# The opening of a two-block transformer kernel: modulation weights into fifteen buffers of their own, bias table first, X scaled for all tiles ahead of the shift

## The reference, cut to what matters

```python
def ada_modulation(c, w, b):                       # w: 1024 x 3072
    mod = jax.nn.silu(c) @ w + b
    shift, scale, gate = jnp.split(mod, 3, axis=-1)
    return shift[:, None], scale[:, None], gate[:, None]

shift, scale, gate = ada_modulation(c, ada_w[layer, 0], ada_b[layer, 0])
h = rms_norm(x, norm_w[layer, 0]) * (1.0 + scale) + shift
y = hybrid_attention_mixer(h, attn_w_in[i], ...)   # h @ w_in, then attention with a bias
x = x + (gate * y)                                 # by distance, taken from rel_bias (32 x 8)
```

## Time and profile before

| | |
|---|---|
| median of 3 runs | 956.2 us (955.88 to 959.43) |
| the profiled execution | 958.09 us, of which its span 956.4 us |
| PE busy | 888.4 us (93%) |
| DVE busy | 692.1 us (72%) |
| ACT busy | 456.8 us (48%) |
| DMA engines | mean 206 GB/s |

### The profile page before, as it was taken

How to read it: one execution, slowest core, us unless ns; L and a number is a source line. 1 busy time by engine, 2 the same in 40 slices (tenths; PEclk the granted TensorE clock), 3 DMA queues, 4 the chain that set the end, 5 groups by cost and what they waited for, 6 DMA issues and landing times.

```text
span 956.4 us, 17671 instructions
## 1 busy us (share of the span) xinstructions
PE 888.4 (93%) x7028; PEld 852.6 (89%) x7028; DVE 692.1 (72%) x877; ACT 456.8 (48%) x573; POOL 58.0 (6%) x104
## 2 busy tenths in 40 slices
PE   2599999899999996799999999999999999999996
PEld 1388879799999996699999999988989999999996
DVE  4889878788878888766666556855487877776665
ACT  2347464566643333456663433444465444444445
POOL 2110110211111110000000000000000000000000
PEclk9789999999999996799999999999999999999998
DMA  9895755499989994057765555653435555654531
GB/s 336 300 339 193 244 200 177 130 319 322 317 306 330 330 316 134 23 184 234 239 199 176 175 183 168 197 166 130 157 90 177 177 179 187 218 173 158 169 126 44
DMA packets 156600, 196.60 MB, mean 206 GB/s; under 512 B 5341, under 2 KB 143116, under 8 KB 156556
## 3 DMA queue, kind: packets, MB, share of 16 engines
q1 hardware_dynamic: 142732, 145.64, 47.6%
q0 software_dynamic: 13824, 50.34, 14.4%
HBM read 194.90 MB, written 1.06 MB: 205 GB/s over the span
## 4 chain that ended last, share of the span: by engine, by line
PE 81%; DVE 9%; ACT 4%; issue 2%; DMA 2%; SPq 1%; DVEq 0%; ACTq 0%
PE G L557 15%; PE G L558 15%; PE G L559 15%; PE A L557 7%; PE A L559 7%; PE A L558 7%; DVE w_lo L1123 2%; ACT w_hi L1786 2%; PE G L632 2%; PE A L685 2%; PE G L633 2%; PE G L634 2%; DMA sinks<-in_attn_sinks_dram 1%; DMA MIX<-bias_rows 1%; DVE HN L1285 1%
## 5 line engine op out<-in xcount | busy, mean ns | idle before, releaser
L1123 DVE TENSOR_TENSOR w_lo<-raw,w_hi 128x2048 fp32r<-128x2048 f32 x135 | 307.1, 2275 | 163.7 <-ACT w_hi L1786 163.5
L1786 ACT ACTIVATE w_hi<-raw 128x2048 fp32r<-128x2048 f32 x135 | 256.6, 1901 | 265.7 <-PE A L559 132.4
L557 PE MATMUL G<-h_hi,w_hi 128*128 128x256 f32 x880 | 257.9, 293 | 22.5 <-DVE h_lo L1268 13.0
L558 PE MATMUL G<-h_lo,w_hi 128*128 128x256 f32 x880 | 253.3, 288 | 0.0
L559 PE MATMUL G<-h_hi,w_lo 128*128 128x256 f32 x880 | 253.2, 288 | 0.0
L557 PEld LDWEIGHTS G<-h_hi,w_hi 128*128 128x128 f32 x880 | 173.0, 197 | 29.5 <-issue 22.5
L558 PEld LDWEIGHTS G<-h_lo,w_hi 128*128 128x128 f32 x880 | 173.6, 197 | 0.2 <-issue 0.2
L559 PEld LDWEIGHTS G<-h_hi,w_lo 128*128 128x128 f32 x880 | 173.2, 197 | 0.0
L557 PE MATMUL A<-u_hi,w_hi 128*128 128x256 f32 x512 | 143.4, 280 | 0.7 <-DVE w_lo L1123 0.7
L558 PE MATMUL A<-u_lo,w_hi 128*128 128x256 f32 x512 | 142.9, 279 | 0.0
L559 PE MATMUL A<-u_hi,w_lo 128*128 128x256 f32 x512 | 142.9, 279 | 0.0
(11 more groups left out here) (325 smaller groups left out, 1315.7 us busy)
## 6 DMA issues: line engine op xcount, KB each, us to landing
raw<-in_mlp_w_dram SPq DMA_DIRECT2D x64, 1024.0 KB, 5.5
ada_raw<-in_ada_w_dram POOLq DMA_DIRECT2D x88, 512.0 KB, 5.7
raw<-in_w_in_dram SPq DMA_DIRECT2D x14, 1024.0 KB, 5.0
raw<-in_w_up_dram SPq DMA_DIRECT2D x11, 1024.0 KB, 5.4
raw<-in_w_gate_dram SPq DMA_DIRECT2D x11, 1024.0 KB, 5.3
raw<-in_attn_w_in_dram SPq DMA_DIRECT2D x9, 1024.0 KB, 7.1
raw<-in_w_down_dram SPq DMA_DIRECT2D x8, 1024.0 KB, 5.2
raw<-in_attn_w_out_dram SPq DMA_DIRECT2D x4, 1024.0 KB, 5.4
```

Source lines behind the costliest of these rows:

```text
L557: pe.matmul(dst, wh, ah, start=start, stop=False)
L558: pe.matmul(dst, wh, al, start=False, stop=False)
L1123: dve.tensor_tensor(w_lo[n % 2][:, 0:k, :], raw[n % RAW][:, 0:k, :], w_hi[n % 2][:, 0:k, :].bitcast(F32), ALU.subtract).then_inc(lo_done, 1)
L1786: act.activation(w_hi[n % 2][:, 0:k, :], raw[n % RAW][:, 0:k, :], ACT.Copy).then_inc(hi_done, 1)
```

## The change

POOL: fifteen slices, 3 to 15 and 19, 20, get buffers of their own, which until then lie idle (Q4, K4, V4, GV, PT, parts of wide, SS, beside the halves of raw). Slice 15 goes to SS, where the table t8 is, so it waits for bias_rows to be written; slice 16 waits until block 1's weights have landed.

SP: rel_bias is the third transfer instead of the eighteenth, bias_rows is issued behind the vectors, and x only behind bias_rows; hankel is issued ahead of block 0, both behind g_raw. PE makes the table second.

DVE: the scaled X goes for all eight tiles into a place of its own, HN0 in wide, between the sums of slices 11 to 14. split_lo(0) and g_lo stand between slices 14 and 15. For the shift, tiles 0 to 3 are summed on ACT and tiles 4 to 7 on DVE; the two have semaphores of their own.

ACT: a new function rows_along sums a bank's four tiles along the row, one ACTIVATE of 128 x 128 with an accumulator each, written back into the bank. It takes the place of DVE's L1174 for scale, for half of the shift, and for gate. g_hi, the copies to BIAS and split_hi(0) now stand behind root(0).

Gate: its transposes move on PE from behind block 2 to behind the attention, its eight sums stand on ACT between high_mix(1) and split_hi(10), its bias on DVE behind split_lo(10).

```diff
-ADA_EARLY = (3, 4, 5, 6, 7, 8, 19, 20)
+ADA_EARLY = (*range(3, 16), 19, 20)
...
-                 for n in range(6)] + [b[:, :, :].rearrange("p t s -> p (t s)") for b in (GE, GG)]
+                 for n in range(5)]
+        early += [b[:, :, :].rearrange("p t s -> p (t s)") for b in (Q4, K4, V4, GV)] + [
+            PT[:, :, :, :].rearrange("p a b s -> p (a b s)"),
+            wide[:, 4:6, :].rearrange("p a b -> p (a b)"), wide[:, 6:8, :].rearrange("p a b -> p (a b)"),
+            SS[:, :, :, :].rearrange("p a b s -> p (a b s)")]
+        early += [b[:, :, :].rearrange("p t s -> p (t s)") for b in (GE, GG)]
...
+        HN0 = wide[:, 0:4, :].rearrange("p a (t s) -> p (a t) s", t=2)
...
-        take_each(("c", 1), ("vecs", 0), ("table", 1), ("x0", 2), ("x1", 3), ("x2", 0), ("x3", 1),
-                  ("ms0", 2), ("scale0a", 3), ("scale0b", 0), ("flip0", 1), ("flip1", 2), ("flip2", 3), ("flip3", 0),
-                  ("shift0a", 1), ("shift0b", 2))
+        take_each(("c", 1), ("table", 0), ("vecs", 3), ("x0", 2), ("x1", 1), ("x2", 0), ("x3", 3),
+                  ("ms0", 2), ("scale0a", 1), ("scale0b", 0), ("flip0", 3), ("flip1", 2), ("flip2", 1), ("flip3", 0),
+                  ("shift0a", 3), ("shift0b", 2))
-                (2, ("glr", "gate0a", *T0[0:3], "kend", *T0[3:5], "ds0", T0[5], "go1", *T0[6:8])),
-                (3, ("vt", "logits", "gate0b", *V0[0:2], "gs1", *V0[2:4], "ds1", "ds2", *V0[4:8]))):
+                (2, ("glr", *T0[0:3], "kend", *T0[3:5], "ds0", T0[5], "go1", *T0[6:8], "gate0a")),
+                (3, ("vt", "logits", *V0[0:2], "gs1", *V0[2:4], "ds1", "ds2", *V0[4:8], "gate0b"))):
...
-                sp.dma_start(x_rows, x[0].rearrange("(k p) d -> p k d", p=P)).then_inc(x_in, 16)
+                sp.dma_start(rb[:, :], rel_bias).then_inc(rb_in, 16)
...
-                sp.dma_start(rb[:, :], rel_bias).then_inc(small_in, 16)
+                bank_was_read(sp, "table")
+                sp.dma_start(scratch.ap(), t8[:, :]).then_inc(table_out, 16)
+                sp.dma_start(x_rows, x[0].rearrange("(k p) d -> p k d", p=P)).then_inc(x_in, 16)
-                bank_was_read(sp, "table")
-                sp.dma_start(scratch.ap(), t8[:, :]).then_inc(table_out, 16)
-                load(N_ATTN, w_in[:, :, ATTN_COLS[0]:ATTN_COLS[0] + COLS])
-                sp.wait_ge(ada_used, 10)
+                load(N_ATTN, w_in[:, :, ATTN_COLS[0]:ATTN_COLS[0] + COLS])
+                sp.wait_ge(early_full[ADA_EARLY.index(2 * DT - 2)], 16)
-                        sp.wait_ge(ada_used, (14, 16, 16)[j - 1])
+                        sp.wait_ge(ada_used, (5, 7, 8)[j - 1])
...
+                if f == 2 * DT - 1:
+                    pool.wait_ge(table_out, 16)
+                if f == 2 * DT:
+                    pool.wait_ge(raw_full[1], 16)
...
-            pe.wait_ge(x_in, 16)
-            turn_x(0)
-            turn_x(1)
+            pe.wait_ge(rb_in, 16)
+            bank_done("table", pe.matmul(bank_empty(pe, "table")[0:HEADS, 0:P], rb[:, :],
+                                         C[0:32, C_HOT:C_HOT + P], start=True, stop=True))
-            pe.wait_ge(small_in, 64)
-            bank_done("table", pe.matmul(bank_empty(pe, "table")[0:HEADS, 0:P], rb[:, :],
-                                         C[0:32, C_HOT:C_HOT + P], start=True, stop=True))
-            turn_x(2)
-            turn_x(3)
+            pe.wait_ge(x_in, 16)
+            for q in range(4):
+                turn_x(q)
...
+            pe.wait_ge(small_in, 48)
...
-            turn_sums(0, "gate", ADA_B)
...
+            turn_sums(0, "gate", ADA_B)
...
+            def with_bias(first, count, col):
+                return dve.tensor_tensor(MOD[:, :, :].rearrange("p m n -> p (m n)")[:, first:first + count],
+                                         mod_sums[:, col:col + count], V[:, V_ADAB + first:V_ADAB + first + count],
+                                         ALU.add)
...
+            src = bank_full(dve, "table")
+            bank_read("table", dve.tensor_copy(t8[:, P:2 * P], src[0:HEADS, 0:P]))
-            src = bank_full(dve, "table")
-            bank_read("table", dve.tensor_copy(t8[:, P:2 * P], src[0:HEADS, 0:P]))
-            ada_next(7)
+            ada_next(6)
+            for half in "ab":
+                bank_was_read(dve, f"scale0{half}")
+            chain(with_bias(DT, DT, DT))
+            chain(factor(0))
+            ssq[0] = 4
+            dve.wait_ge(rstd_ready, 1)
+            for p in range(4):
+                for t in (2 * p, 2 * p + 1):
+                    ins = dve.scalar_tensor_tensor(out=HN0[:, t, :], in0=X[:, t, :], scalar=GAIN[:, 0, t:t + 1],
+                                                   in1=rstd[:, :], op0=ALU.mult, op1=ALU.mult)
+                ins.then_inc(norm_ready, 1)
+                ada_next(1)
+            split_lo(0)
-            chain(part(0, "scale"))
-            factor(0)
-            split_lo(0)
-            ada_next(4)
-            part(0, "shift").then_inc(mod_ready, 1)
+            ada_next(1)
+            src = bank_full(dve, "shift0b")
+            ins = dve.tensor_reduce(part_sums[:, 4:8], src[:, :].rearrange("p (t k) -> p t k", t=4), AX_X, ALU.add)
+            bank_read("shift0b", ins)
+            bank_was_read(dve, "shift0a")
+            dve.tensor_tensor(MOD[:, 0, 0:4], mod_sums[:, 0:4], V[:, V_ADAB:V_ADAB + 4], ALU.add
+                              ).then_inc(mod_ready, 1)
+            bank_was_read(dve, "shift0b")
+            dve.tensor_tensor(MOD[:, 0, 4:8], part_sums[:, 4:8], V[:, V_ADAB + 4:V_ADAB + 8], ALU.add
+                              ).then_inc(shift_ready, 1)
-            ssq[0] = 4
-            norm("n0", 0, GAIN[:, 0, :], MOD[:, 0, 0:DT])
+            for p in range(4):
+                if p == 2:
+                    dve.wait_ge(shift_ready, 1)
+                dve.wait_ge(norm_ready, p + 1)
+                low_pair("n0", p, HN0[:, 2 * p:2 * p + 2, :], shift=MOD[:, 0, 0:DT])
-            ada_next(5)
+            ada_next(2)
-            dve.wait_ge(small_in, 64)
+            dve.wait_ge(small_in, 48)
+            ada_next(1)
...
-            chain(part(0, "gate"))
-            ada_next(1)
+            ada_next(3)
...
+            for half in "ab":
+                bank_was_read(dve, f"gate0{half}")
+            chain(with_bias(2 * DT, DT, 2 * DT))
...
+            def rows_along(bank, col):
+                for t in range(4):
+                    tile = bank[:, t * P:(t + 1) * P]
+                    ins = act.activation(tile, tile, ACT.Copy,
+                                         accum_out=mod_sums[:, col + t:col + t + 1])
+                return ins
...
+            root(0)
+            for half in range(2):
+                src = bank_full(act, f"scale0{'ab'[half]}")
+                bank_read(f"scale0{'ab'[half]}", rows_along(src, DT + 4 * half))
-            split_hi(0)
-            root(0)
+            split_hi(0)
+            src = bank_full(act, "shift0a")
+            bank_read("shift0a", rows_along(src, 0))
-            high_norm("n0", MOD[:, 0, 0:DT])
+            for p in range(4):
+                if p == 2:
+                    act.wait_ge(shift_ready, 1)
+                for t in (2 * p, 2 * p + 1):
+                    ins = act.activation(h_hi[:, t, :], HN0[:, t, :], ACT.Identity, bias=MOD[:, 0, t:t + 1])
+                ins.then_inc(hhi_ready, 1)
...
+            for half in range(2):
+                src = bank_full(act, f"gate0{'ab'[half]}")
+                bank_read(f"gate0{'ab'[half]}", rows_along(src, 2 * DT + 4 * half))
```

More of the change, by code:

```diff
@@ L183, in build @@
         part_sums = sb("part_sums", [P, DT])
+        mod_sums = sb("mod_sums", [P, 3 * DT])
         gate_ps = sb("gate_ps", [P, DT])
@@ L292, in build @@
         ada_full = sems(*(f"ada_full{n}" for n in range(3)))
-        early_full = sems(*(f"early_full{n}" for n in range(8)))
+        early_full = sems(*(f"early_full{n}" for n in range(len(ADA_EARLY))))
+        rb_in = sem("rb_in")
         hi_done, lo_done, block_used, ada_used = sems("hi_done", "lo_done", "block_used", "ada_used")
@@ L305, in build @@
         e5_hi, e5_ready = sems("e5_hi", "e5_ready")
+        shift_ready = sem("shift_ready")
         pool_done = sem("pool_done")
```

## The result

The kernel after takes 963.8 us (median of 5 runs, 962.9 to 965.3) against 956.2 (5 runs, 955.73 to 959.43): 1.0065 times as long, 95% interval [1.0045, 1.0085]. The forecast was 958.2, with a range of 951 to 961: the kernel is slower, as forecast, but by some three times as much, and the time lies outside the range. The profiled execution took 963.80, its span on the page is

The account below looks back on a forecast made before the run. The prediction took the opening's wait for hankel's data, then PE's nearly gapless chain, as the bound. +0.8 (block 0) - 0.9 (gate transposes) + 2.15 (block 10) = +2.05 us gave 958.2 us, range 951 to 961.

Parts of the forecast that it names:

- The sum, +0.8 - 0.9 + 2.15: Whole kernel: block 0, gate's transposes and the wait at block 10 add to +2.05 us, median 958.2.
- term for block 0: Opening: block 0 starts later, its pairs follow faster, the clock starts at 1.2 GHz; its end moves by +0.8 us.
- Hankel's landing, 33.3: Opening: hankel lands at 33.3 us instead of 36.87, behind g_raw, as the queues alternate packet by packet.
- the w_hi wait on DVE: Opening: DVE finishes slice 14 at about 38 and idles until 42 for block 0's w_hi, ahead of split_lo(0).
- the copies: Opening, ACT: copies to BIAS end at 40.4, 7.1 us behind hankel's landing as before; split_hi(0) follows.
- the start of block 0: PE: the first matmul of block 0 at 50.7 us, 2.3 later than before.
- The faster rival: Opening: g_raw gets through early and does not hold hankel; 954.1 to 951.6 us in all, chance 0.26.
- slice 15 behind split_lo(0): Opening, DVE: slice 15 follows split_lo(0) and g_lo, takes 1.35 us and ends at 46.25, ahead of PE's shift transposes.
- slices 16 to 18 ("Nothing"): Weights of blocks 1 to 3 and slices 16 to 18 arrive before they are wanted: no cost.
- transposes -0.9: Gate: eight transposes leave PE's chain in the attention, 0.87 us less; behind the attention they cost nothing.
- sums +2.15: Gate: eight sums on ACT take 2.7 us ahead of split_hi(10); less 0.55 slack, PE waits 2.15 at block 10.
- Scale on ACT, costed at nothing: Opening: scale's reduction moves from DVE, 1.41 us, to ACT, 3.1; DVE waits about 3 us, covered by 4.

Follow-up runs that it names:

- e3: The kernel after with gate's sums behind split_hi(10) and slices 21 to 23 summed at their old places: ratio 1.0043 to the kernel before.
- e7: e3 with mod_sums also allocated last in the attention's scope, so that no other buffer moves: ratio 1.0017 to the kernel before.
- e12: The kernel before with 96 unused bytes per partition ahead of u_hi, u_lo, late_acc, and ahead of f_hi, f_lo, only: ratio 1.0027.
- e5: The kernel before with an unused buffer of 96 bytes per partition behind part_sums, moving all later buffers: ratio 1.0037.
- e8: e7 with hankel and block 0 issued ahead of g_raw, and g_hi behind split_hi(0) on ACT: 958.89 us, ratio 1.0016 to the kernel before.
- e15: e7 with slice 15 added on DVE ahead of split_lo(0) and g_lo: 955.13 us, ratio 0.9974 to the kernel before.
- e2: The kernel after with slices 21 to 23 summed on DVE where they were before: ratio 1.0046 to the kernel before.
- e6: The kernel after with mod_sums allocated last in the attention's scope, no instruction changed: ratio 1.0034 to the kernel before.
- e11: The kernel after with mod_sums declared as 128 bytes per partition instead of 96: ratio 1.0065 to the kernel before.
- b1: The kernel before again, only a comment changed: ratio 1.0009.
- e4: e2 with the gate also finished where and as before, on PE and DVE: ratio 1.0058 to the kernel before.
- e9: The kernel before with an unused buffer of 32 bytes per partition behind part_sums: ratio 1.0013.
- e10: The kernel before with an unused buffer of 128 bytes per partition behind part_sums: ratio 1.0008.
- e13: The kernel before with 96 unused bytes per partition between u_lo and late_acc, moving late_acc only: ratio 1.0003.
- e16: e15 with matmuls nobody reads on PE, six behind scale's transposes and four behind the shift's: 952.96 us, ratio 0.9952 to the kernel before.
- e14: The kernel before with only the gate finished late: transposes behind the attention, reductions and bias on DVE behind split_lo(10): 957.0 us, ratio 0.999.
- e17: e14 with matmuls nobody reads on PE, eight behind scale's transposes and four behind the shift's: 957.38 us, ratio 0.9996 to the kernel before.

## Why the prediction was wrong

**The steps that failed.** The sum, +0.8 - 0.9 + 2.15, ends at block 10 ("block 10 and all behind it shift") and passes over the attention's sums: it puts at nothing, without a reason, the down projections, where the runs show 2.5 to 3.5 us for the place of the buffers (e3 to e7, e12, e5), and the moved sums, 1.37. Its term for block 0 was formed against a base that came late by chance: +0.8, where the kernels differ by 2.5.

**Hankel's landing, 33.3:** 33.1, right, by turns of single packets, and the w_hi wait on DVE (2.82 us ahead of split_lo(0)), the copies (end 39.1; 40.4 forecast), the start of block 0 (49.6; 50.7) came in order. The Trainium skill, "DMA: Bandwidth & Descriptors", section "Queues, rings and completion order", has whole packets of 9 to 17 descriptors per turn; by that g_raw would have been through early. The trace does not agree, and it decides: it counts 546 against 544 packets in 5 us while one queue moved 4 KB rows (1.98 MB, 3.6 KB a packet) and the other 64-byte rows (0.03 MB), g_raw landed at 30.7, and hankel where the count of rows puts it. The faster rival made g_raw the obstacle; e8 shows that without it hankel's own rows take its place.

**Block 0, +0.8: failed by its base.** The way through the new opening was foreseen well: first matmul at 50.7 and, with +0.8, first reader at 59.0; the means of the nine profiles are 50.6 and 58.7. But I made the difference to one profiled execution whose opening was the latest of eight: 48.44 and 58.22, where the means are 47.1 and 56.2. So the term is +2.5, and the -0.88 of the pair of profiles is luck, since after's opening is the earliest of its nine (its clock rose at 53.5, 3.9 us behind the first matmul, where I had 5.6 to 7.8). The wait that decides was in the prediction too, slice 15 behind split_lo(0), but only as a part of the way and not as the price of an order that could be otherwise; e15 gives it 4.1 us.

**The moved sums: not priced at all.** I looked at slices 16 to 18 ("Nothing") and not at slices 21 to 23 in the attention, two of which now stand with slice 24 ahead of unit 3's bias: +1.37, gone in e2.

**The new buffer: not considered.** I costed instructions, and mod_sums has none of its own cost; its 96 bytes move the operand that PE streams: 3.0 us at the landmarks, 3.5 in e5. This is the largest term that was missing.

**Gate, transposes -0.9, sums +2.15.** -0.84 and +2.0 against this profile of before, by the mechanism foreseen: w_hi(10) starts behind the sums. The price was 2.26 (eight at 0.28, from 144.82 to 147.08), not 2.7. The agreement of the second number is in part luck. PE waited 1.16 us ahead of block 10 and not 2.15, because block 9 ran at a lower clock and took the rest (in e2, at a clock of 1.00, the wait is 1.75). With the sums there the stretch is 2.0 to 2.1 longer than in before in all four profiles (after, e2, e6, e11), whatever the clock, since w_lo(10) ends it. But in the eight profiles with the gate finished as before (before, b1, e4, e5, e9, e10, e12, e13) it is longer too, by 0 to 2.15, on average 1.1. Over kernels the sums cost about 0.9. The Trainium skill, "ScalarE: Activation LUTs", section "Step-by-step: what each stage is for", calls PSUM the faster destination for ScalarE. No run here isolates that: the row of 0.39 in the earlier trace rows reads from SBUF, and the one that reads PSUM takes 0.27 to SBUF, where rows_along takes 0.26 to PSUM.

**Scale on ACT, costed at nothing,** held in after: DVE waited 4.55 us for it at 25 to 30 and still was done with slice 14 before w_hi(0) came. In e15 and e16 that cover shrinks to 1.3 us and to nothing: there this wait is next on the path.

**Sum.** +2.05 forecast, +5.7 in the pair of profiles: 3.0 (place of buffers) and 1.37 (sums) were missing, 1.7 less came at block 0, and 0.8 is the clock at 150 to 200, in which the profile of before is the exception. Over kernels: opening 2.5, places 3.0, moved sums 1.4, transposes -0.85, gate's sums 0.9 make 7.0; the ratio gives 6.2 (0.0065 x 956.2), with an interval from 4.3 to 8.1, and the two medians, of five runs each, are 7.6 apart. Between neighbours the whole times give e14 -1.0, e7 over e14 +2.6, e3 over e7 +2.5, after over e3 +2.1. The last is less than the 3.4 of the two orders at their landmarks; each of these steps is known to 1 or 2 us only, and that difference is not settled.

## What to carry to other kernels

Price the declarations too: a new small buffer goes behind those that PE streams, or its effect is measured alone with an unused buffer in the old kernel. Where a transfer is brought forward, look at what its engine does next: here 2.4 us won at hankel became 3.6 us lost at the start of block 0 (49.59 against 45.95 in e14), by one sum that stood behind a split waiting for ACT. And compare a profile's landmarks with several executions before a term of 1 us is built on them: eight profiles with one and the same opening differ by up to 3.4 us at block 0.

## What the hardware showed that I had not expected

The same 48 matmuls of a block at full clock, with PE never idle, take 5.60 us with their moving operand in its old place in SBUF (5.65 in two of ten profiles) and 5.70 or 5.76 with it 96 bytes further (seven profiles). Work whose result nobody reads makes a kernel faster: ten matmuls of 128x512 in PE's idle stretches take 2.1 us off (e16 against e15), since flips and block 0 then run at full clock; twelve in the old opening won nothing (e17). A row sum of 128x128 on ACT, in place in PSUM, is issued every 0.28 us with its accumulator read.
